# A hybrid block on one core: inputs returned by quarters, a scan shared by two engines, the gated product inside the attention stretch, and a chunk inverse from commuting factors

## The reference, cut to what matters

```python
# first block
o = diff_attention(q1, q2, k1, k2, vh, lam)            # causal, 4 heads
x_re, x_im = lax.associative_scan(combine, (ar, ai, bu_re, bu_im), axis=1)[2:]
y = einsum(x_re, c_re) - einsum(x_im, c_im) + d_skip * u
y = gelu(y)
y = y * sigmoid(y @ w_glu + b_glu)
y = rms_norm(y, ssm_out_g)
h_res = h_res + rms_norm(concat([o, y]) @ w_out, post_mix_g)
h_res = h_res + rms_norm((silu(h @ w_gate) * (h @ w_up)) @ w_down, post_ffn_g)
# second block: proj = norm(x) @ w_in; retention; RWKV-7:
def step(state, inp):
    r_t, w_t, k_t, v_t, kk_t, b_t = inp
    sa = einsum('bhvk,bhk->bhv', state, -kk_t)
    state = state * w_t + sa[..., None] * b_t + v_t[..., None] * k_t
    return state, einsum('bhvk,bhk->bhv', state, r_t)
# then x += mixed @ w_o; a second feed-forward; a gated per-layer input; a last norm
```

## Time and profile before

| what | value |
|---|---|
| median of 3 runs | 3672.29 us (3667.94 to 3681.34) |
| the profiled execution: its own time | 3670.09 us |
| its span, first to last instruction | 3668.3 us |
| PE busy | 3158.4 us (86%) |
| DVE busy | 1767.3 us (48%) |
| ACT busy | 947.7 us (26%) |
| POOL busy | 1973.4 us (54%) |
| granted TensorE clock, mean | 0.920 |

### The profile page before, as it was taken

One profiled execution on the slowest core, in us unless ns is written; L12 is line 12 of the kernel. 1 busy time (PEld: TensorE's weight loads), 2 busy tenths in 40 slices (PEclk: granted clock), 3 DMA queues, 4 the chain that ended last, 5 costly groups with the idle time before them and its releaser, 6 DMA issues.

```text
span 3668.3 us, 47977 instructions
## 1 busy us (share of the span) xinstructions
PE 3158.4 (86%) x19536; PEld 2439.6 (67%) x19536; DVE 1767.3 (48%) x2367; ACT 947.7 (26%) x1665; POOL 1973.4 (54%) x1076
## 2 busy tenths in 40 slices
PE   5996496599998768988899997998899998799997
PEld 4674364476776556766677775677677776687885
DVE  6623833344443552566556554285556555422233
ACT  3111022332332232122233323313233332300012
POOL 4720222255455464755566655574666665568773
PEclk9887697799999888999999998999999999899998
DMA  4334133222222234322222223432222221322321
GB/s 139 105 98 75 33 100 116 69 68 77 75 69 66 89 118 135 122 78 75 67 76 67 82 100 124 139 108 64 80 77 75 75 87 64 121 92 92 98 93 63
DMA packets 154412, 325.76 MB, mean 89 GB/s; under 512 B 34417, under 2 KB 71473, under 8 KB 154193
## 3 DMA queue, kind: packets, MB, share of 16 engines
q1 hardware_dynamic: 58752, 213.94, 18.3%
q10 hardware_dynamic: 95440, 108.76, 9.6%
HBM read 279.78 MB, written 42.86 MB: 88 GB/s over the span
## 4 chain that ended last, share of the span: by engine, by line
PE 71%; DVE 18%; ACT 4%; ACTq 2%; DMA 2%; issue 2%; DVEq 0%
PE ps L1712 29%; PE ps L1741 12%; PE ps L1753 11%; PE ps L1943 2%; PE ps L1572 2%; DVE acc_dense L2130 2%; PE ps L1452 1%; DVE ffh_lo L2804 1%; DVE act_lo L2130 1%; PE ps L1482 1%; DVE local L2130 1%; PE ps L1492 1%; ACTq L898 1%; DVE added L2130 1%; DVE rq L2130 1%
## 5 line engine op out<-in xcount | busy, mean ns | idle before, releaser
L530 POOL TENSOR_TENSOR w_hi<-w_raw,ones 128x1024 fp32r<-128x1024 f32 x408 | 806.7, 1977 | 1396.3 <-DMA w_raw<-weights 1381.8
L532 POOL TENSOR_TENSOR w_lo<-w_raw,w_hi 128x1024 fp32r<-128x1024 f32 x408 | 1003.2, 2459 | 32.0
L1712 PE MATMUL ps<-act_hi,w_hi 128*128 128x512 f32 x1696 | 707.8, 417 | 6.5 <-DVE act_lo L2130 6.5
L1712 PE MATMUL ps<-act_lo,w_hi 128*128 128x512 f32 x1696 | 681.8, 402 | 0.0
L1712 PE MATMUL ps<-act_hi,w_lo 128*128 128x512 f32 x1696 | 676.6, 399 | 0.0
L1712 PEld LDWEIGHTS ps<-act_hi,w_hi 128*128 128x128 f32 x1696 | 326.6, 193 | 100.0 <-issue 17.0
L1712 PEld LDWEIGHTS ps<-act_hi,w_lo 128*128 128x128 f32 x1696 | 325.9, 192 | 75.9
L1712 PEld LDWEIGHTS ps<-act_lo,w_hi 128*128 128x128 f32 x1696 | 326.2, 192 | 67.4 <-issue 1.7
L2130 DVE TENSOR_TENSOR acc_dense<-acc_dense,ps 128x512 f32<-128x512 f32 x352 | 242.0, 688 | 243.5 <-PE ps L1741 185.2
L1741 PE MATMUL ps<-w_hi,ffh_hi 128*128 128x512 f32 x704 | 297.8, 423 | 67.1 <-DVE acc_dense L2130 65.9
L634 ACT ACT_TABLE_LOAD x204 | 261.7, 1283 | 301.7 <-PE ps L1712 100.2
(11 more groups left out here) (389 smaller groups left out, 4573.2 us busy)
## 6 DMA issues: line engine op xcount, KB each, us to landing
w_raw<-weights SPq DMA_DIRECT2D x408, 512.0 KB, 3.5
rw<-rw_t ACTq DMA_DIRECT2D x24, 256.0 KB, 2.3
rw<-lora_t ACTq DMA_DIRECT2D x24, 256.0 KB, 2.0
row<-x ACTq DMA_DIRECT2D x8, 512.0 KB, 3.5
row_dense<-x ACTq DMA_DIRECT2D x8, 512.0 KB, 3.6
res<-row_dense ACTq DMA_DIRECT2D x8, 512.0 KB, 2.6
row_mix<-res ACTq DMA_DIRECT2D x8, 512.0 KB, 7.2
res<-row_mix ACTq DMA_DIRECT2D x8, 512.0 KB, 3.4
```

What stands on the lines that cost most here:

```text
L530: pool.tensor_tensor(w_hi[:, s], raw, ones[:, 0:1].to_broadcast([P, 1024]), MUL).then_inc(w_hi_made, 1)
L532: pool.tensor_tensor(w_lo[:, s], raw, w_hi[:, s].bitcast(F32), SUB).then_inc(w_ready, 1)
L1712: mm = pe.matmul(out, ws[w][:, s, P * k:P * k + P], acts[a][:, k, x], start=(k, w, a) == (0, 0, 0), stop=(k, w, a) == (KT - 1, 1, 0))
```

## The change

Four things are changed.
1. **Inputs by quarters.** `load_inputs(m)` brings back one quarter of u with 8 transfers of 16x8x130, issued when the next quarter's last product is done (quarters 0 to 2) and after the first far value product (quarter 3). The states start at n = 13 instead of 18, PE waits for the quarter that it needs, and the table `gt` is loaded just ahead of them.
2. **Scan by pairs.** DVE scans 10 of the 16 pairs in 13 parts (n = 21 to 33). POOL scans the other 6 with the same operations on narrower tiles (48 on 128x120, 36 on 128x12, 24 on 128x216), between splits of weights. `ssm_scanned` now has to reach 2. The outputs come every 3 steps (n = 38 to 59).
3. **Gated product inside.** `glu(0)` runs its four parts at n = 60, 63, 65 and 67, in tiles that lie over u_in and the states (`glu_at[0]`), and in PSUM banks 2 and 3. Phase 1 starts with the attention step and 8 dense pieces; the number of dense pieces is as before. PE waits for `glu_root` before the third dense piece.
4. **Inverse from commuting factors.** (I+X)(I+X^2)(I+X^4)(I+X^8) is formed as a product of two products. The levels are 16 + 16 + 8 + 16 + 8 products of 64x64, which is one level more with the same 64 products, and a tile has 14 steps instead of 13. Sides lie in two PSUM banks so that ACT can take both with one 128x512 copy.

The diff, cut to its core:

```diff
-    SCAN_PARTS = 11
+    SCAN_PARTS = 13
+    VECTOR_PAIRS = 10
...
+    def glu_tiles(h):
+        at = (ARENA, AT_MIX)[h]
+        tiles_at = [place(f"y_raw_{h}", [P, 4, OCT, BANK // OCT], F32, at)]
+        for n, (name, dt) in enumerate((("yh", F32R), ("yl", F32R), ("ysq", F32), ("sig", F32))):
+            tiles_at.append(place(f"{name}_{h}", [P, 4, BANK], dt, at + 8192 * (n + 1 if h or n < 2 else 2 * n - 3)))
+        tiles_at.append(place(f"rinv_{h}", [P, BANK], F32, at + (40960 if h else 16384)))
+        return tiles_at
+
+    glu_at = [glu_tiles(0), glu_tiles(1)]
+    glu_bank = lambda h, m: 4 + m if h else 2 + m % 2
     glu_vec = small[:, 192:200]
...
-        "mm": ("toks", "pairs", "sq0", "kv", "sq1", "sq2", "sq3", "z0", "m0", "z1", "m1", "wu", "parts", "step0", "step1"),
-        "dve": ("nt", "nx", "adds", "xt1", "xt2", "inv2", "inv3", "m0", "m1", "fold", "st1", "st0"),
-        "act": ("toks", "xp1", "kv", "xp2", "xt3", "it0", "it1", "wu", "y"),
+        "mm": ("toks", "pairs", "sq0", "kv", "sq1", "sq2", "sq3", "sq4", "z0", "m0", "z1", "m1", "wu", "parts", "step0", "step1"),
+        "dve": ("nt", "nx", "adds", "sums", "inv3", "m0", "m1", "fold", "st1", "st0"),
+        "act": ("toks", "x1", "kv", "x2", "uv", "it0", "it1", "wu", "y"),
...
-        extra = [[]] * 18 + [["ssm"]] * (TB + SCAN_PARTS + 2) + ([[]] * 3 + [["ssm"]]) * (TB - 1)
-        early = 14
+        events, done, early = ["heads"] + ["far"] * 8, 8, 14
+        states, scan, outputs = 13, 21, 38
+        at = [states + b for b in range(TB)] + [scan + n for n in range(SCAN_PARTS)] + [outputs - 1] + [outputs + 3 * b for b in range(TB)]
+        gated = (60, 63, 65, 67)
...
+            events += ["heads"] + ["far"] * (now - done) + ["ssm"] * at.count(n) + ["glu"] * gated.count(n)
...
+        own = slice(VECTOR_PAIRS, PAIRS)
+        owned = PAIRS - VECTOR_PAIRS
+        own_tmp = lambda n: [scan_tmp[1][:, a, 0:n] for a in range(2)]
+
+        def scan_within(steps):
+            x = xs[:, :, own, 1:NOCT + 1].rearrange("p r q (i j) -> p r q i j", j=RUN)
+            now, other = [a.rearrange("p (r q i) -> p r q i", r=2, q=owned) for a in own_tmp(2 * owned * BLOCKS)]
+            factor = lambda a: a_step[:, a, :, own].unsqueeze(3).to_broadcast([P, 2, owned, BLOCKS])
+            for j in steps:
+                mul(now, x[:, :, :, :, j - 1], factor(0))
+                mul(other, x[:, ::-1, :, :, j - 1], factor(1))
+                mul(now, now, other, op=ADD)
+                mul(x[:, :, :, :, j], x[:, :, :, :, j], now, op=ADD)
+
+        def scan_ends():
...
+        split_to(20)
+        pool.wait_ge(ssm_x, TB)
+        pool.wait_ge(factors_ready, 2)
+        for part in range(3):
+            scan_within(range(1 + 4 * part, 5 + 4 * part))
+            split_to(21 + part)
+        scan_ends()
+        for n in range(owned // 2):
+            scan_spread(VECTOR_PAIRS + 2 * n, n == owned // 2 - 1)
+            split_to(25 + n)
...
+                    if s == 1 and m:
+                        load_inputs(m - 1)
...
-                        spills_landed(0, 1)
-                        for e in range(OCT):
-                            act.dma_start(u_in[SG * e:SG * e + SG], t["u_scratch"][:, :, e, :].rearrange("m (g h) c -> h (m g) c", h=SG)).then_inc(ssm_landed, 16)
-                        load_input_factors(0)
+                        load_inputs(3)
...
+        def load_inputs(m):
+            spills_landed(m % 2)
+            act.wait_ge(ssm_landed, 16 * (6 + OCT * m))
+            for e in range(OCT):
+                act.dma_start(u_in[SG * e:SG * e + SG, 8 * m:8 * m + 8], t["u_scratch"][m, :, e, :].rearrange("(g h) c -> h g c", h=SG)).then_inc(ssm_landed, 16)
...
+                if b == 0:
+                    spills_landed(0, 1)
+                    load_input_factors(0)
...
-                rw_kept(v, "sq0", xp[:, :, :], units(bank(2, 0, 256)), "xp1")
...
+                rw_kept(v, "sq0", by_side, ps[:, 6:8, 0:256], "x1")
...
+                rw_kept(v, "sq1", by_side_next, ps[:, 6:8, 0:256], "x2")
+                yield
+                yield
+                act.wait_ge(rw_mm, nth("mm", "sq3", v))
+                give(fn(uv[:, 0:3].rearrange("p k j n -> p (k j n)"), bank(2, 0, 3 * P), ACT.Copy), act_step)
+                mark(fn(uv[:, 3].rearrange("p j n -> p (j n)"), bank(3, 0, P), ACT.Copy), rw_act, nth("act", "uv", v))
...
+        heads, far, gated = attention(0), project_far(), glu(0)
         for side in HEAD_EVENTS:
-            next({"heads": heads, "ssm": states, "far": far}[side])
+            next({"heads": heads, "ssm": states, "far": far, "glu": gated}[side])
...
-                    pe.wait_ge(ssm_landed, 16 * (6 + OCT))
+                pe.wait_ge(ssm_landed, 16 * (6 + OCT * (b // 2 + 1)))
...
+                        if (h, j, uu, k) == (0, 0, 0, 2):
+                            pe.wait_ge(glu_root, 1)
...
+        def side_products(lhs, rhs, at, before, after):
+
+            for j in range(2):
+                for side in range(2):
+                    for c in range(2):
+                        rows = head(c ^ side * before)
+                        mm = pe.matmul(ps[head(c ^ side * after), 6 + side, at + CH * j:at + CH * j + CH], lhs(rows, side, j), rhs(rows, side, j), start=True, stop=True)
+            return mm
...
-            pe.wait_ge(rw_dve, nth("dve", "xt1", v))
-            pe.wait_ge(rw_act, nth("act", "xp1", v))
-            chunk_products(3, xp, xt[1])
-            chunk_products(2, xt[1], xp)
-            mark(chunk_products(1, xt[1], inv), rw_mm, nth("mm", "sq1", v))
+            pe.wait_ge(rw_act, nth("act", "x1", v))
+            side_products(of_side(zi, 1), of_side(zi, 0), 0, 1, 0)
+            mark(side_products(of_side(zi, 0), of_side(zi, 1), P, 1, 0), rw_mm, nth("mm", "sq1", v))
...
-            pe.wait_ge(rw_dve, nth("dve", "xt2", v))
-            pe.wait_ge(rw_act, nth("act", "xp2", v))
-            chunk_products(3, xp, xt[0])
-            mark(chunk_products(1, xt[0], inv), rw_mm, nth("mm", "sq2", v))
+            pe.wait_ge(rw_act, nth("act", "x2", v))
+            mark(side_products(of_side(zi_next, 0), of_side(zi_next, 1), 0, 0, 1), rw_mm, nth("mm", "sq2", v))
 
         def rw_level3(v):
-            pe.wait_ge(rw_dve, nth("dve", "inv2", v))
-            pe.wait_ge(rw_act, nth("act", "xt3", v))
-            mark(chunk_products(2, xt[1], inv), rw_mm, nth("mm", "sq3", v))
+            pe.wait_ge(rw_dve, nth("dve", "sums", v))
+            side_products(of_side(zi_next, 1), of_units(xt), 0, 0, 1)
+            for side in range(2):
+                for j in range(2):
+                    for c in range(2):
+                        at = P * (1 + side) + CH * j
+                        mm = pe.matmul(ps[head(c), 6, at:at + CH], zi[head(c), side, 0, j], inv[head(c), 2 * side + j], start=True, stop=True)
+            mark(mm, rw_mm, nth("mm", "sq3", v))
+
+        def rw_level4(v):
+            pe.wait_ge(rw_act, nth("act", "uv", v))
+            mark(side_products(lambda rows, side, j: uv[rows, 3 * side, j], lambda rows, side, j: uv[rows, 1 + side, j], 0, 1, 0), rw_mm, nth("mm", "sq4", v))
 
         def rw_off_product(v, n):
...
-            for part in range(4):
-                scan_within(range(1 + 3 * part, 4 + 3 * part))
+            for part in range(6):
+                scan_within(range(1 + 2 * part, 3 + 2 * part))
...
-            mark(dve.tensor_copy(xt[1][:, :, :], units(bank(3, 0, 256))), rw_dve, nth("dve", "xt1", v))
+            tt(xt[:, :, :], xt[:, :, :], identities(4), ADD)
 
         def rw_level1(v):
             dve.wait_ge(rw_mm, nth("mm", "sq1", v))
-            tt(inv[:, :, :], inv[:, :, :], units(bank(1, 0, 256)), ADD)
-            mark(dve.tensor_copy(xt[0][:, :, :], units(bank(3, 0, 256))), rw_dve, nth("dve", "xt2", v))
-
-        def rw_add_to_inverse(v, stage, b, mark_as):
-            dve.wait_ge(rw_mm, nth("mm", stage, v))
-            tt_mark(inv[:, :, :], inv[:, :, :], units(bank(b, 0, 256)), ADD, rw_dve, nth("dve", mark_as, v))
+            tt(zi[:, :, 0], zi[:, :, 0], identities(2, 2), ADD)
+
+        def rw_level2(v):
+            dve.wait_ge(rw_mm, nth("mm", "sq2", v))
+            units_of_sides = inv[:, :, :].rearrange("p (s j) n -> p s j n", s=2)
+            tt(units_of_sides, ps[:, 6:8, 0:P].rearrange("p s (j n) -> p s j n", j=2), identities(2, 2), ADD)
+            tt_mark(zi_next[:, :, 1], zi_next[:, :, 1], identities(2, 2), ADD, rw_dve, nth("dve", "sums", v))
+
+        def rw_level4(v):
+            dve.wait_ge(rw_mm, nth("mm", "sq4", v))
+            mark(dve.tensor_copy(inv[:, :, :].rearrange("p (s j) n -> p s (j n)", s=2), ps[:, 6:8, 0:P]), rw_dve, nth("dve", "inv3", v))
 
         def rw_merged(v, n):
...
```

More of the change, by code:

```diff
@@ L497, in build @@
         for step, n in zip(mix, FILLS[phase]):
[L498 removed]
+            ORDER += [(h, u) for u in step]
             EVENTS[phase].append(("mix", len(ORDER)))
@@ L585, in mixing @@
                     rw_keys(v + 1)
```

(27 more changed lines are left out.)

131 lines of the change are left out of this document (74 added, 57 removed).

## The result

| kernel | median us | ratio to before, with its 95% interval |
|---|---|---|
| before | 3679.11 (3667.94 to 3681.34, 5 runs) | 1 |
| after | 3651.09 (3643.87 to 3652.30, 5 runs) | 0.9932 (0.9906 to 0.9957) |

The forecast was 3651, from a median before of 3672 in 3 runs; over 5 runs that median is 3679, and the ratio puts the change at 25 us. The profiled execution has a span of 3645.8 us, 22.5 less than before, where the sum said 21. But the parts do not agree with the terms, as the rows show.

A forecast was written before the change was run, and what follows sets the result against it. PE's own work bounds the RWKV stretches; DVE's scan, a table wait and the gated-product chain bound the head events. Terms 14 - 8 + 18 - 3 give 21 us less: 3649 profiled, 3651 median, range 3640 to 3662.

The forecast's parts named there:

- What bounds the stretches: PE's own work bounds both RWKV stretches; in the head events DVE's scan, a 24.3 us table wait and the gated-product chain.
- PE has 64 small products per tile before and after: In the inverse, PE's product count stays the same; the whole inverse term was 3 us more, from DVE.
- PE's own work bounds them: In the two RWKV stretches PE is the limit, and only 61 us of gaps can be won.
- The prediction's own sign of being wrong: Among its listed signs of failure: the RWKV stretches change by over 10 us.
- The fifth level: The inverse's extra level in each RWKV tile was costed at 0; uncovered, 45 us; slower rival 3696, chance 0.10.
- The rival that RWKV's gaps shrink: In RWKV, DVE leaves two levels of the inverse, so up to 20 us of gaps return: 3628, chance 0.11.
- Inputs by quarters: Before the states, PE's 24.3 us table wait falls to 10, winning 14 us, bounds 4 to 20.
- Two engines meet: In the scan, DVE pays half for POOL's narrow tiles, 19 us, plus 18 beside splits; the stretch gets 8 longer.
- its own end: POOL's scan work ends in 93 us, under DVE's 105, so costed at 0; up to 15 if weights delay it.
- The prediction's own rule: At the gated product it looked at what stands behind ACT's 15.4 us of issues: an attention exponential and the norms.
- Gated product: Between step 60 and phase 1's first score, starting the chain with step 60 wins 18 us, bounds 5 to 28.
- attention stalls and follows in the gaps of the chain; that adds some 3: Beside the 54.7 us gated-product chain, attention held behind ACT's issues costs only some 3 us.

The follow-up runs named there:

- e7: The kernel before with inputs by quarters and the new inverse, scan on DVE alone, outputs every 4 steps: 3626.28 us, ratio 0.9868.
- e1: The kernel before with the new inverse alone (5 levels, 14 steps per tile): 3640.6 us, ratio 0.9913.
- e6: The kernel before with quarters, scan by pairs and new inverse, gated product outside, outputs every 4 steps from n = 38: 3623.76 us, ratio 0.9860.
- e3: The changed kernel with the gated product outside, at the head of phase 1 as before; outputs every 3 steps: 3645.61 us, ratio 0.9923.
- e11: The changed kernel with outputs every 4 steps from n = 34 and the gated product's parts at 63, 64, 65, 67: 3638.36 us, ratio 0.9909.
- e12: Quarters, scan by pairs and new inverse, gated product outside, outputs every 4 steps from n = 34 instead of 38: 3638.41 us, ratio 0.9902.
- e2: The changed kernel with the inverse of before, the other three parts kept: 3679.12 us, ratio 1.0013.
- e9: The changed kernel with each product of the new inverse reading and writing the same half of the rows: 3663.42 us, ratio 0.9976.
- e8: The changed kernel with the first part of the gated product one step later, at n = 61: 3651.82 us, ratio 0.9929.

## Why the total was right and its terms were not

| term | predicted us | measured us, by ratios |
|---|---|---|
| inputs by quarters | -14 | -16 (e7 to e1) |
| scan by pairs | +8 | -3 (e6 to e7) |
| outputs every 3 steps for 4 | no term | +23 (e3 to e6) |
| gated product inside | -18 | +3 (after to e3), +3 (e11 to e12) |
| inverse | +3 | -32 (e1) |
| sum | -21 | -25 |

"e7 to e1" is e7's ratio less e1's, and so on. The five differences form one chain from the kernel before to the kernel after, so their sum must come out at what the whole change measured. It doesn't show that the parts add up in another order.

The predicted 3651 is met by luck: 48 us of unforeseen gain (35 in the inverse, 11 in the scan, 2 in the quarters) nearly cancel 44 of unforeseen loss (23 in the outputs, 21 in the gated product). The scan's and the gated product's measured values lie within what two ratios can tell from nothing; the quarters, the outputs and the inverse do not. Taken by its steps:

- **What bounds the stretches** was right for the head events and for phase 2. That is why the failed step matters: "PE has 64 small products per tile before and after". Their count was read, their rate was not, and PE saves 29 ns on 56 of them. Both rates stood in the trace before: 8 such products in 0.46 us from start to end where all four pairs of halves are used, 8 in 0.63 to 0.68 in the inverse. For phase 3 "PE's own work bounds them" fails in part: PE's busy time fell there by 8 us and the stretch by at most 3. The prediction's own sign of being wrong, an RWKV stretch that changes by over 10 us, came in phase 2.
- **The fifth level** lies under the dense pieces, as costed: PE's waits for the inverse's own tiles (zi_next) are 2.8 us in phase 2. The rival that RWKV's gaps shrink (3628, chance 0.11) came true in phase 2 and not in phase 3, where PE's gaps grew. In phase 2 PE's wait for acc_dense is 25.8 us before and 24.4 in e2, and 14.6, 12.1 and 9.4 in the kernel after, in e1 and in e9. It goes with the new inverse and not with the halves. Whether it is DVE's one operation less or the dense pieces spread over 14 steps was not tried.
- **Inputs by quarters**: mechanism and size right (13.2 us of waiting left for 10).
- **Two engines meet**: DVE is slowed beside POOL, as costed, and the size was too large. DVE pays 0.22 us in a step of scan_within, 3 us in twelve, for 48 x 0.22 = 10.6. The scan takes 90.2 us (343.1 to 433.3) for 89.0 (357.3 to 446.3), 1 more for 8, and in e6 90.3 for e7's 87.2, 3 more; POOL ends at 433.0, so its own end costs nothing, as costed. The Trainium skill's lock for a whole instruction ("SBUF — State Buffer", section "SBUF: two separate sides") would have DVE wait for the end of POOL's operation, some 0.5 us long, each time that this began first; with narrow tiles the trace shows 0.05 us per operation, and DVE's two products at 345.48 run while POOL's two at 345.76 do, so for them the trace does not agree.
- **The outputs' spacing** had no term, although the change names it. I read the queue of ACT at three places and not at an output. The prediction's own rule, to ask what is queued behind the 9 issues, would have shown it.
- **Gated product**: the step that failed is "attention stalls and follows in the gaps of the chain; that adds some 3". The chain grew by 13.3 us. From step 60's first score to phase 1's first score there are 79.5 us in the kernel after (557.19 to 636.66), where the prediction had 64. In e3 there are 93.8 (552.98 to 646.74) with 8 dense pieces more on the way, which took 13.5 us in the kernel before: the chain starts 20 us earlier and nothing is left of it. e8 shows that the place of the issues beside one exponential isn't why the chain grew; what made it grow stays open.

## What to carry to other kernels

Price small matmuls by their start-to-start rate in the trace and count how many fall to each pair of input and output half, since the same number of products can cost half as much PE time. When periodic work goes into a repeating sequence, give it the sequence's period and look at what stands behind its issues at its place: one step was worth 56 us here, more than the waits it made, because the clock fell behind them. A total that comes out right proves none of its terms; changing one part at a time tests them. Lay the traces over each other by work done before crediting a saving to a stage: 8 us less of PE's work in phase 3 brought 0 to 3.

## What the runs showed of the hardware

- 64x64 products in float32 start every 58 ns when they use two pairs of halves and every 29 ns when they use four. In the three orders tried a level of 16 products on four pairs takes 0.63 to 0.68 us.
- Waits of 3.8 to 4.3 us on PE, once per 24 us, came with a granted clock of 0.74 over 150 us, where nearly the same work without them took 110 us at 0.94.
- DVE and POOL, with tiles of 200 and 120 columns side by side, slow DVE by some 0.05 us per operation, by the sum of a step against the estimate for it alone; beside POOL's 2.4 us splits the whole rest of the split was paid.
- The version to use is e6 (e7, without the scan by pairs, can't be told from it): quarters, scan by pairs and the new inverse, the gated product left outside, outputs every 4 steps from n = 38: 3623.76 us, 0.9860 (0.9839 to 0.9880) of the kernel before.
